# TensorE's loops over the MLP blocks written out as straight code

## The reference

```python
x = x + concat(mixer(z_mix), memattn(z_mem)) @ w_out[l]
h2 = rmsnorm(x, norm2[l])
x = x + square(relu(h2 @ w_mlp1[l])) @ w_mlp2[l]     # 1024 -> 4096 -> 1024
```

## Time and profile before

| | |
|---|---|
| time before, median of 3 runs | 1305.91 us (1302.9 to 1310.01) |
| profiled execution | 1303.68 us |
| its span, first to last instruction | 1301.8 us |
| TensorE matmuls busy | 1227.4 us, 94% |
| VectorE busy | 588.4 us, 45% |
| ScalarE busy | 408.8 us, 31% |
| GpSimd busy | 357.4 us, 27% |
| mean granted TensorE clock | 0.98 |
| data moved | 132.87 MB, 102 GB/s |

### The profile page before, as it was taken

One profiled execution on the slowest core, in us unless ns is written; L12 is line 12 of the kernel. 1 busy time (PEld: TensorE's weight loads), 2 busy tenths in 40 slices (PEclk: granted clock), 3 DMA queues, 4 the chain that ended last, 5 costly groups with the idle time before them and its releaser, 6 DMA issues.

```text
span 1301.8 us, 23305 instructions
## 1 busy us (share of the span) xinstructions
PE 1227.4 (94%) x9556; PEld 1169.0 (90%) x9556; DVE 588.4 (45%) x867; ACT 408.8 (31%) x754; POOL 357.4 (27%) x290
## 2 busy tenths in 40 slices
PE   6997999999999999999999888699999999999994
PEld 5876999999999999998899655699999999998994
DVE  6777444323333333456534878545333332333334
ACT  6444332212212112343412466433212211211221
POOL 3363024205305205320063200013502502502524
PEclk9999999999999999999999989699999999999997
DMA  7613322222222222222344456022222222222211
GB/s 271 229 67 96 130 89 90 82 96 84 84 95 81 96 81 81 85 93 67 130 117 133 164 183 211 1 69 94 84 95 82 83 96 83 81 98 69 96 50 69
DMA packets 37050, 132.87 MB, mean 102 GB/s; under 512 B 4226, under 2 KB 5122, under 8 KB 36322
## 3 DMA queue, kind: packets, MB, share of 16 engines
q1 hardware_dynamic: 35858, 123.42, 27.6%
q0 software_dynamic: 1104, 8.15, 2.1%
HBM read 121.18 MB, written 7.03 MB: 98 GB/s over the span
## 4 chain that ended last, share of the span: by engine, by line
PE 88%; DVE 7%; ACT 2%; issue 1%; DMA 0%; DVEq 0%; POOL 0%; SPq 0%; ACTq 0%
PE psum L433 80%; DVE inv_rms L1048 1%; DVE weights_split L1029 1%; PE psum L579 1%; PE psum L486 1%; PE psum L477 1%; ACT weights_split L772 1%; DVE tiny L1136 1%; PE psum L561 1%; PE psum L535 1%; PE psum L515 1%; PE psum L519 0%; DVE probs_heads L1115 0%; PE psum L541 0%; PE psum L504 0%
## 5 line engine op out<-in xcount | busy, mean ns | idle before, releaser
L433 PE MATMUL psum<-operand_b,weights_split 128*128 128x272 f32 x4416 | 562.9, 289 | 9.4 <-DVE weights_split L1029 6.2
L433 PEld LDWEIGHTS psum<-operand_b,weights_split 128*128 128x128 f32 x4416 | 556.8, 189 | 13.9 <-issue 7.2
L433 PE MATMUL psum<-operand_a,weights_split 128*128 128x272 f32 (+1 forms) x4116 | 528.2, 290 | 25.6 <-DVE weights_split L1029 19.7
L433 PEld LDWEIGHTS psum<-operand_a,weights_split 128*128 128x128 f32 x4116 | 521.9, 190 | 30.5 <-issue 23.1
L772 ACT ACTIVATE weights_split<-weights_raw 128x1024 fp32r<-128x1024 f32 (+1 forms) x186 | 192.9, 1037 | 411.6 <-PE psum L433 411.6
L1029 DVE TENSOR_TENSOR weights_split<-weights_raw,weights_split 128x1024 fp32r<-128x1024 f32 (+1 forms) x186 | 239.6, 1288 | 136.4 <-ACT weights_split L772 136.3
L1414 POOL TENSOR_TENSOR squares<-staging 128x544 f32<-128x544 f32 x64 | 76.4, 1194 | 476.2 <-ACT operand_a L818 213.9
L1083 DVE TENSOR_TENSOR residual<-psum,residual 128x544 f32<-128x544 f32 x48 | 34.8, 725 | 176.0 <-PE psum L433 176.0
L1064 DVE SCALAR_TENSOR_TENSOR staging<-psum,inv_rms 128x544 f32<-128x544 f32 x56 | 40.6, 725 | 156.4 <-PE psum L433 156.4
L1407 POOL TENSOR_TENSOR squares_sum<-squares_sum,squares 128x544 f32<-128x544 f32 (+1 forms) x35 | 48.6, 1388 | 115.7 <-ACT squares L784 115.1
L1416 POOL TENSOR_TENSOR operand_a<-squares,operand_a 128x544 fp32r<-128x544 f32 x32 | 65.0, 2032 | 2.5
(11 more groups left out here) (203 smaller groups left out, 732.6 us busy)
## 6 DMA issues: line engine op xcount, KB each, us to landing
weights_raw<-in_weights SPq DMA_DIRECT2D x180, 512.0 KB, 3.6
cache_tiles<-in_page_k SPq DMA_DIRECT2D x16, 384.0 KB, 4.0
cache_tiles<-in_page_v SPq DMA_DIRECT2D x16, 384.0 KB, 3.8
cache_tiles<-in_mem_k SPq DMA_DIRECT2D x8, 512.0 KB, 5.2
cache_tiles<-in_mem_v SPq DMA_DIRECT2D x8, 512.0 KB, 5.9
residual<-in_x SPq DMA_DIRECT2D x1, 2176.0 KB, 12.2
out_y<-projected SPq DMA_DIRECT2D x8, 272.0 KB, 2.1
rotated<-projected POOLq DMA_DIRECT2D x4, 408.0 KB, 7.1
```

Of the source, the lines that this page charges most:

```text
L433: mm = pe.matmul(ps[:, 2 * (j % PS) + hf, 0:n], w(wr), act[:, ar, k, hf * n:(hf + 1) * n], start=(q == 0 and wr == 0 and ar == 0), stop=(q ...
```

## The change

The loop `pe.Fori` over blocks 1 to 3 becomes a Python loop, so that the three blocks are written out in TensorE's program, in both calls of `mlp`. The index `i` and the unit number `u` are then plain numbers, and all waits are on constants. The program of the other engines stays as it is.

```diff
                 block_(0, u0, True)
-                with pe.Fori(1, BLOCKS) as i:
-                    block_(i, i * (2 * KT) + u0, False)
+                for i in range(1, BLOCKS):
+                    block_(i, u0 + 2 * KT * i, False)
```

## The result

The changed kernel takes 1295.6 us (median of 13 runs, 1290.64 to 1299.64) against 1304.19 us (13 runs, 1299.06 to 1310.01). The ratio is 0.9936, 95% interval 0.9918 to 0.9954: 8.3 us less by the ratio, somewhere between 6.0 and 10.7 (the two medians lie 8.6 us apart). I had forecast 6.3 us less and a median of 1299.6 us. Of the 4.0 us by which that median is too high, 1.7 us are the starting point: I counted from 1305.91 us, the median of three runs.

What follows compares the result with a forecast made beforehand. TensorE, busy for 94% of the span, was taken as the bound. Only the second MLP's two slow branches counted, all other terms being 0: 1305.9 - 6.3 = 1299.6 us, range 1293 to 1306.

Steps and rivals of the forecast that it cites:

- Two jumps miss and two hit: TensorE's loop branches: removing the first MLP's two gives 0, being hidden; removing the second MLP's two gives 6.29 us.
- It is the loop's place against the pieces: Second MLP's loop begins close to the end of a 16 KB code piece, reaching into one more than the first's.
- The eighth piece takes the head's place: In the second MLP, the body's last 16 KB code piece displaces the one holding the loop's start, so the branch waits.
- The two losses, 2.92 + 3.37 = 6.29 us: Two long passes of the second MLP's loop, 99.21 and 99.66 us; writing them out saves 6.29 us.
- Registers' arithmetic, hidden: Computing awaited values in TensorE's loops: removing it gives 0, at the most 0.24 us.
- More code to fetch, free: TensorE's written-out passes raise q8's count from 70 to about 76; cost taken as 0, upper bound 79 us.
- a gap that moves: Rival: two code pieces in the written-out passes come late, giving back 6.3 us; 1305.9 us, chance 0.15.
- a slower kernel: Rival: at least five of some 25 code fetches in the written-out passes come late; 1315 us, chance 0.06.
- The rival of four losses: Rival: the first MLP's branches also miss in ordinary executions, so 4 x 3.15 = 12.6 us go; 1293.3 us, chance 0.12.

Runs made afterwards that it cites:

- heads at 0: Kernel before with both TensorE loops kept, each loop's first instruction moved to instruction 0 of a 256-instruction code piece: 1295.86 us, ratio 0.9942.
- heads at 230: Kernel before with both TensorE loops kept, each loop's first instruction moved to instruction 230 of a 256-instruction code piece: 1314.16 us, ratio 1.0089.
- The hit at 210 and the miss at 219: Kernel before with loops kept, first MLP's loop starting at instruction 210 of a code piece, second MLP's at 219: one execution, 1304.09 us.
- The run with the hint: Kernel before with both TensorE loops kept and their backward branches announced by hint_back_edge=True: 1298.89 us, ratio 0.9954.

## Why the prediction was right

- **Two jumps miss and two hit: shown.** The first MLP written out alone gives nothing, the second alone everything.
- **It is the loop's place against the pieces: shown.** Both loops hit with heads at 0 and both miss with heads at 230. The hit at 210 and the miss at 219 put the limit where a count of eight pieces has it, each in one of the MLPs.
- **The eighth piece takes the head's place: half right.** The count is right as a limit. The run with the hint shows no fetch just ahead of the branch, and no miss. So it is the piece fetched ahead that does the harm.
- **The two losses, 2.92 + 3.37 = 6.29 us: too small.** This is the term that was off. It was read from one execution in which the clock didn't fall behind the gap, and I took that one for the usual case. Three profiles of the kernel before give 6.3, 7.3 and 7.7 us, 7.1 on the mean; all seven loops that missed give 7.4. The measured 8.3 us has an interval down to 6.0 us, so both are within it; whether the rest of about 1 us is more than scatter isn't settled.
- **Registers' arithmetic, hidden: right.** The same seven units of block 1 of the first MLP, written out, take 383.71 - 341.62 = 42.09 us, against 42.10 in the loop. The kernel with heads at 0 keeps all that arithmetic and lies at 0.9942, the changed one at 0.9936, with intervals that overlap nearly wholly.
- **More code to fetch, free: right.** q8 has the 76 packets that were forecast, and both MLPs stay whole. No written-out piece came late, which was the ground for the rivals of a gap that moves and of a slower kernel. The ground that I gave against the slower kernel was too broad: both MLPs together have 128 units, not over 130 of straight code. Straight were the 32 of the two blocks 0, and 32 more were first passes of the loops that fetched their code.
- **The rival of four losses** (1293.3 us, all jumps missing in ordinary executions) has a time inside the measured range, but its mechanism is refuted: writing out the first MLP alone changes nothing (ratio 1.0004, at the least 0.9985, which leaves no room for 6.3 us). With it falls the rule of the Trainium skill (Runtime: NRT & Kernel Launch, Instruction fetch mechanics) that only two pieces are at hand: a body that spans seven is jumped back over in 0.2 us with no fetch (no row of q8 from 374 to 582 us). That page's other figure, 128 KiB of instruction memory for TensorE in blocks of 16 KiB, agrees with the limit found, seven pieces of body and one fetched ahead.
- The forecast of 0.48% less lay just under the line of 0.5%, with a chance of 0.46 for more than that and 0.48 for less. The measured 0.64%, with an interval from 0.46% up, falls on the far side. The clock behind the gap, had I known of it, would have moved the forecast across.

## What to carry to other kernels

A long loop isn't dear by itself. Look at the duration of its backward branch: 0.2 us is hidden by the sequencer's lead, 4 us is a fetch of code and shows as a gap, whatever engine the view of waits names. If it misses, writing out is one cure; moving the loop's head within its piece does the same with a third of the loop's code. Such a miss comes and goes with any edit that shifts code ahead of the loop, so a change of some tenths of a percent elsewhere in such a kernel should be read together with its branches.

When a gap of 2 us sits in a stretch in which TensorE is otherwise never idle, price it from several executions: the clock may fall behind it in most and not in the one that you look at.

## What the runs showed of the hardware that was not expected

- A limit this sharp: a body of 1578 instructions jumps back in 0.2 us with its head at instruction 210 of a piece (first MLP) and in 4.0 to 4.3 us with it at 219 (second MLP).
- A gap of some 2 us on TensorE was followed by 3.4 us at half the clock (0.91 over 20 us) at the first missed jump of six loops out of seven, and never at the second. In the two repeats of the kernel before, the two missed passes together lasted 1.0 and 1.4 us longer than in the first profile.
- A branch hint executed a whole pass of 96 us ahead of its branch works: 51 code packets instead of 70, no miss.
